# Unread padding in on-chip memory: where the two operands of a split float32 product begin

## What is computed

```python
hx = rmsnorm(x, norm_w[l]) * (1.0 + scale_x[:, None, :]) + shift_x[:, None, :]
(fx, fgx, nqx, nkx, nvx, ngx, gqx, gkx, gvx, ggx, zfx, zbx) = jnp.split(hx @ w_in[l], IN_SPLITS, axis=-1)
...
mix_x = jnp.concatenate([four_x * jax.nn.silu(fgx), na_x * jax.nn.silu(ngx), gla_x * jax.nn.silu(ggx)], axis=-1)
x_new = x + gate_x[:, None, :] * (mix_x @ w_out[l])
```

```python
z = jnp.einsum('bsd,de->bse', a, w_in[i])
...
h = h + jnp.einsum('bse,ed->bsd', mixed, w_out[i])
gate = jax.nn.sigmoid(jnp.einsum('bsd,de->bse', _rmsnorm(h, g_ple[i]), w_ple_gate[i]) + b_ple_gate[i])
h = h + gate * jnp.einsum('bsp,pd->bsd', p[i], w_ple_proj[i])
```

## Time and profile before

| | |
|---|---|
| median of 3 runs | 4333.1 us (4327.89 to 4334.98) |
| span of the profiled execution (first to last instruction) | 4326.4 us |
| TensorE matmuls busy | 3967.8 us, 92% of the span |
| TensorE weight loads busy (beside the matmuls) | 3241.8 us, 75% |
| VectorE, ScalarE, GpSimd busy | 2036.2, 1432.6, 683.4 us (47%, 33%, 16%) |
| DMA moved | 525.90 MB, mean 122 GB/s |

### The profile page before, as it was taken

How to read it: one execution, slowest core, us unless ns; L and a number is a source line. 1 busy time by engine, 2 the same in 40 slices (tenths; PEclk the granted TensorE clock), 3 DMA queues, 4 the chain that set the end, 5 groups by cost and what they waited for, 6 DMA issues and landing times. The chain is left out here.

```text
span 4326.4 us, 66533 instructions
## 1 busy us (share of the span) xinstructions
PE 3967.8 (92%) x25359; PEld 3241.8 (75%) x25359; DVE 2036.2 (47%) x4616; ACT 1432.6 (33%) x3255; POOL 683.4 (16%) x761
## 2 busy tenths in 40 slices
PE   6999999899679799999999869799999989979799
PEld 4777789777568688778977658677777867868687
DVE  5365111167656542111127567632750456657554
ACT  5000444256422310144327523321111467721211
POOL 3021000223120210000032220131430001000100
PEclk8999999999889899999999989899999989989899
DMA  5244221731256422222273345432111143357221
GB/s 195 90 147 143 82 77 61 230 136 59 100 196 220 175 100 73 95 76 77 75 240 106 113 146 198 173 112 90 64 71 66 47 134 102 103 214 255 79 77 64
DMA packets 215264, 525.90 MB, mean 122 GB/s; under 512 B 27478, under 2 KB 88392, under 8 KB 205604
## 3 DMA queue, kind: packets, MB, share of 16 engines
q1 hardware_dynamic: 188740, 438.91, 29.2%
q0 software_dynamic: 26208, 82.74, 5.4%
HBM read 330.43 MB, written 191.13 MB: 121 GB/s over the span
## 5 line engine op out<-in xcount | busy, mean ns | idle before, releaser
L72 PE MATMUL tm_tacc<-tm_tw_hi,hT_hi 128*128 128x384 f32 (+1 forms) x1120 | 414.6, 370 | 17.2 <-DVE tm_tw_lo L906 10.0
L73 PE MATMUL tm_tacc<-tm_tw_lo,hT_hi 128*128 128x384 f32 (+1 forms) x1120 | 410.0, 366 | 0.0
L74 PE MATMUL tm_tacc<-tm_tw_hi,hT_lo 128*128 128x384 f32 (+1 forms) x1120 | 410.0, 366 | 0.0
L72 PE MATMUL tz_tacc<-tz_tw_hi,hT_hi 128*128 128x512 f32 x896 | 359.4, 401 | 6.0 <-POOL tz_tw_lo L935 4.1
L72 PE MATMUL cm_acc<-hT_hi,cm_wb_hi 128*128 128x512 f32 (+1 forms) x912 | 362.2, 397 | 0.0
L73 PE MATMUL tz_tacc<-tz_tw_lo,hT_hi 128*128 128x512 f32 x896 | 355.0, 396 | 0.0
L74 PE MATMUL tz_tacc<-tz_tw_hi,hT_lo 128*128 128x512 f32 x896 | 355.0, 396 | 0.0
L74 PE MATMUL cm_acc<-hT_hi,cm_wb_lo 128*128 128x512 f32 (+1 forms) x912 | 344.3, 378 | 0.0
L73 PE MATMUL cm_acc<-hT_lo,cm_wb_hi 128*128 128x512 f32 (+1 forms) x912 | 343.9, 377 | 0.0
L788 DVE SCALAR_TENSOR_TENSOR tm_ds<-tm_dg,tm_ds 128x512 f32<-128x512 f32 (+1 forms) x40 | 25.6, 639 | 532.1 <-ACT tm_ds L782 532.1
L72 PEld LDWEIGHTS tm_tacc<-tm_tw_hi,hT_hi 128*128 128x128 f32 x1120 | 210.9, 188 | 59.1 <-DVE tm_tw_lo L906 13.6
(11 more groups left out here) (405 smaller groups left out, 8770.1 us busy)
## 6 DMA issues: line engine op xcount, KB each, us to landing
scr_z<-tz_tz SPq DMA_DIRECT2D x112, 256.0 KB
scr_zcm<-cm_zo SPq DMA_DIRECT2D x96, 256.0 KB, 2.0
scr_ztm<-tm_tz SPq DMA_DIRECT2D x68, 256.0 KB, 2.0
scr_xres<-out_x POOLq DMA_DIRECT2D x34, 512.0 KB, 4.1
cm_area<-in_w_ada POOLq DMA_DIRECT2D x64, 256.0 KB, 3.0
scr_z<-out_xn POOLq DMA_DIRECT2D x32, 512.0 KB, 4.8
mo_z<-scr_z SPq DMA_DIRECT2D x16, 1024.0 KB
tz_traw<-in_w_in SPq DMA_DIRECT2D x7, 2048.0 KB, 8.4
```

Of the source, the lines that this page charges most:

```text
L72: nc.tensor.matmul(out, ah, bh, start=start, stop=False)
L73: nc.tensor.matmul(out, ah, bl, start=False, stop=False)
L74: return nc.tensor.matmul(out, al, bh, start=False, stop=stop)
```

## The change

Three kinds of unread buffers are allocated, each a few dozen to 256 bytes per partition, so that later buffers begin elsewhere. `pad_to` pads until the next buffer begins a wanted number of bytes above the other operand, modulo 512: 256 everywhere, but 96 in `tz`. `edge` moves the buffers at the right-hand end down by 96 bytes, which brings `wo_lo` to the residue of `wo_hi`. No instruction is added, removed or moved, on any engine, and no transfer.

```diff
+LINE = 512
+EDGE = 96
+
+
+def residue(nc):
+
+    return (nc.sbuf_base + 31) // 32 * 32 % LINE
+
+
+def pad_to(nc, name, at, apart=256):
+
+    gap = (at + apart - residue(nc)) % LINE
+    if gap:
+        nc.alloc_sbuf_tensor(f"{name}_pad", [128, gap // 4], F32)
+
...
-    def __init__(self, alloc, name, shape):
+    def __init__(self, alloc, name, shape, at=None):
+        self.at = at
...
     raw = [P.sb(f"raw{j}", [128, KC, 128]) for j in range(2)]
+    pad_to(nc, f"{P.name}_wb", hT.at)
     wb = [Split(P.sb, f"wb{j}", [128, KC, 128]) for j in range(2)]
...
     raw, w_in = first.raw, first.w_in
+    pad_to(nc, f"{P.name}_tw", hT.at, 96 if turn else 256)
     wb = Split(P.sb, "tw", [128, KC, width])
...
         right = lambda n, shape: self.nc.alloc_sbuf_tensor(f"{P.name}_{n}", shape, F32, side="right")
+        right("edge", [128, EDGE // 4])
...
+            nc.alloc_sbuf_tensor(f"wl{l}_edge", [128, EDGE // 4], F32, side="right")
             self.lo_rows = [nc.alloc_sbuf_tensor(f"wo{l}_lo{j}", [128, LT], F32R, side="right") for j in range(KC // 2)]
...
+        self.at = residue(nc)
         self.hi = P.sb("hi", [128, KC, D], F32R)
...
+        pad_to(nc, f"{P.name}_mT", wo.at)
         mT = [Split(P.sb, f"mT{j}", [128, KC, 128]) for j in range(2)]
...
+        pad_to(nc, f"{P.name}_hT", fw.wo.at)
         hT = [Split(P.sb, f"hT{j}", [128, KC, 128]) for j in range(2)]
```

More of the change, by code:

```diff
@@ L2430, in __init__ @@
     def __init__(self, P):
-        self.wo = Split(P.sb, "wo", [128, KC, D])
+        self.wo = Split(P.sb, "wo", [128, KC, D], residue(P.nc))
         self.raw_in = [P.sem(f"raw_in{j}") for j in range(2)]
@@ L3146, in second_block @@
     with nc.cleanup_on_exit():
-        hT = Split(nc.alloc_sbuf_tensor, "hT2", [128, KC, LX])
+        hT = Split(nc.alloc_sbuf_tensor, "hT2", [128, KC, LX], residue(nc))
         order = [2, 3, 0, 1, 4, 5, 6]
@@ L3176, in first_layer @@
         with nc.cleanup_on_exit():
-            hT = Split(nc.alloc_sbuf_tensor, f"hT_{l}", [128, KC, LT])
+            hT = Split(nc.alloc_sbuf_tensor, f"hT_{l}", [128, KC, LT], residue(nc))
             with phase(nc, f"cm{l}") as P:
```

## The result

The changed kernel takes 4303.08 us (median of 4 runs, 4300.26 to 4307.91) against 4334.04 for the kernel before (4 runs, 4327.89 to 4336.56). The ratio is 0.9934, 95% interval 0.992 to 0.9948: 31 us or 0.7% faster, within 0.3% of the 4291 us forecast, with 11 us less gain than the 41.9 of the sum. The profiled execution of after is its slowest run (4307.91, span 4306.1), that of before its fastest (4327.89, span 4326.4).

A forecast was written before the change was run, and what follows sets the result against it. The prediction took TensorE's matmul stream as the bound; gains of 7.6 + 10.8 + 7.2 + 5.1 + 2.3 + 8.9 = 41.9 us took 4333.1 to 4291.2 us. The range over the cases was 4218 to 4346.

The forecast's parts named there:

- What bounds: Stages with split products: only TensorE's matmul stream sets the time, so a nanosecond per matmul is one of the kernel.
- That the distance of the starts makes the pace: Split products: the distance between both operands' starts sets the pace, as 6.6 ns between the two layers of `cm`.
- nothing changes: Rival, all stages: starts don't matter, something else such as VectorE's traffic parts the `cm` layers; 4333 us, chance 0.20.
- my form of it: Split products: the next matmul's weight load and the running matmul's stream hinder each other reading on-chip memory; no separate size.
- 226.7 at 256: Split products of 512 columns: distance 256 runs at 226.7 ns, the best level of the trace, chosen between 220.1 and 233.3.
- a level further down: Rival, split products: 256 removes one more step, pace 220.1 ns; 108.5 us gained, 4225 us, chance 0.22.
- Slower: Rival, split products: 256 is like its neighbour 224, all stages at 233.3 ns; 13.5 us lost, 4346.6 us, chance 0.20.
- `tm`, `out`, `mo`: These stages reach 226.7 ns at 512 columns: 10.8, 7.2 and 5.1 us gained; 384 columns in `tm` gain 0.
- `tz`: Stage `tz`, at its new distance: between nothing and a full level of 17.7 us; the middle, 8.9 us, taken.
- `cm` of layer 0: `cm`, layer 0: 1152 matmuls gain 6.6 ns each, 7.6 us.
- `fin`: Stage `fin`: 704 matmuls go from 230.0 to 226.7 ns, 2.3 us; the small `plT` products left out.
- The likeliest case: All stages: best level of the trace, 226.7 ns at 256; 4291 us, own range 4271 to 4300, chance 0.38.

The follow-up runs named there:

- only_tz0: Kernel before with 64 unread bytes ahead of the moving operand in `tz` alone, bringing it to distance 0: 4319.65 us, ratio 0.9974.
- tz0: Changed kernel with distance 0 instead of 96 bytes in `tz`: 4290.42 us, ratio to the kernel before 0.9899.
- both_moved: Kernel before with every left-hand buffer 96 bytes further on, distances kept except for `wo_lo` in `out`: 4339.27 us, ratio 1.0013.
- the two sweeps: Changed kernel with other distances of the operands' starts in each stage, dealt differently in two kernels: 4335.75 and 4338.29 us, one run each.
- low_half: Changed kernel with 320 unread bytes between the halves of `mT` in `out` and `mo`, low half at distance 64: 4312.53 us.
- half_load: Changed kernel with `mo` at distance 224 and 64 of 128 stationary columns loaded for six of eight slices in `out` and `mo`: 4297.31 us.
- fine: Changed kernel with the stationary operand further on by 4 and 8 bytes in `out` (layers 0, 1), 16 in `mo`, 24 in `fin`: 4306.97 us.

## Why the prediction was right, step by step

- **What bounds: right.** TensorE's stream set the end. `only_tz0` turned 17.7 us of pace into 12.4 us of kernel time, `tz0` into 15.5.
- **That the distance of the starts makes the pace: right, and shown** by `both_moved` (addresses change, paces stay), by `only_tz0` (one distance, one stage) and by the two sweeps. VectorE's traffic, which the rows could not exclude, is excluded by them: the stages keep their instructions and change their pace. With this the rival *nothing changes* has fallen. The Trainium skill says in "TensorE: Matmul & The Clock Gate", Step-by-step, that the two operands have independent read ports and that a load takes nothing from the stream. If that were all, there would be no place for 6.6 ns per matmul that hang on the distance of the two starts alone, and the measurement decides. *How* the two accesses meet, in a port or elsewhere, isn't shown: `low_half` refuted my form of it, `half_load` and `fine` fit neither theory.
- **226.7 at 256: right to a tenth of a ns, for half a reason.** I chose it because the distances on both sides of 256, 192 and 0, were good. The sweeps show that the period is 256, so that 256 is the same distance as 0, which rows 6 had already priced. The rival *a level further down* had no room after that: there is no farthest distance at 256. *Slower* compared 256 with its neighbour 224, on a curve where a neighbour says nothing.
- **`tm`, `out`, `mo`: right** in pace, and 1.7, 1.4 and 0.6 us short in time. That 384 columns were already one level lower held in most of the stream, 173.3 at 256 too, but not in all: the earlier trace rows missed the stretches at 176.7. By my estimate from the traces, 267 and 513 such matmuls in the two profiles of before at 3.4 ns each, some 1.3 of the 9.1 us of `tm` come from them and not from 512 columns.
- **`tz`: the step that failed.** I wrote that nothing decides between nothing and a level, and took the middle, 8.9 us. Measured: 0.1. With the period of 256 known, 416 is 160, and rows 5 gave its price, 233.3. The mean of `out` at 231.1 misled me, because it mixes distances of 0 and 416 over three matmuls. As `low_half` showed, one bad operand out of three gives the same mean of 231.1: it costs 4.4 ns on the mean of three, not a third of 6.6.
- **`cm` of layer 0: 7.6 forecast, 2.8 seen.** The pace is there. By the unrounded starts of the first profile of each kernel, intervals up to 260 ns add up to 7.2 us less, and the longer ones to 3.0 more; 8 intervals went over from the first kind to the second. Part of these are the matmuls of the row sums, which wait for VectorE. The groups of before and then of after, 90 to 470 us (in the idle column, DVEq is VectorE's sequencer):

```profile
L328 PE MATMUL cm_msums<-cm_mones,cm_area 128*128 128x1 f32 x64 | 7.7, 250 | 1.4 <-DVEq L353 1.4
L319 PE MATMUL cm_msums<-cm_area,cm_mpick 128*2 128x512 f32 x8 | 4.1, 596 | 2.4 <-DVEq L353 2.4
```

```profile
L345 PE MATMUL cm_msums<-cm_mones,cm_area 128*128 128x1 f32 x64 | 7.7, 250 | 1.8 <-DVEq L370 1.8
L336 PE MATMUL cm_msums<-cm_area,cm_mpick 128*2 128x512 f32 x8 | 4.1, 592 | 3.6 <-DVEq L370 3.6
```

  The two waits go from 3.8 to 5.4 us, and in the second pair of profiles from 3.9 to 5.3: VectorE did not get faster, so a matmul that comes earlier waits longer for it. That is 1.6 of the 3.0 us; the rest has no name.
- **`fin`: 2.3 forecast, 5.1 seen.** With `hT` 24 bytes off, at 230.0, `fine` has 255.3 us in this stage against 251.6, so 3.7 us hang on that distance. From start to start the products of `hT` give 3.3 us (177.3 to 174.0), 1 more than the pace alone. Those of `plT`, which I had left out, changed their distance as well and give 1.1 (41.0 to 39.9), and the wait ahead of the transposes gives the 0.3 to 0.8 that are left.
- **The sum.** The stages give 27.0 us where 41.9 were forecast: 8.8 is `tz`, 4.8 `cm` of layer 0, 0.3 `cm` of layer 1, 3.8 are `tm`, `out` and `mo`, and `fin` returned 2.8. The medians differ by 31 and 26 us in the two comparisons.

The likeliest case held, though its own range (4271 to 4300) missed the time by 3 us. That `tz0` lands at 4290, on the forecast, is chance: it has 17.7 us of pace in `tz` where the forecast had 8.9, and less elsewhere.

## What to carry to other kernels

Where matmuls follow each other without a gap, divide the distance of two starts by the matmuls between them; the mean duration hides a difference of 3%. If two stages with the same shapes have different paces, compare where their two operands begin, modulo 256 here, before looking at anything that moves, and try distance 0, measured at your own number of columns, since at 256 columns another one was better. 32 to 256 unread bytes per stage were worth 1% of this kernel. And when a table of prices over some parameter is rough, look for its period before choosing a value between neighbours.

## What the runs showed of the hardware

- The pace of 128x128 by 128x512 split products depends on the distance of the operands' starts modulo 256 bytes: 226.7 ns at 0; 228.9 to 230.0 at 192; 231.5 to 234.3 at 32, 64, 96, 128, 160 and 224. At 384 columns it is 173.3 at 0, 96 and 192, 175.9 at 128, and at 224 either 173.3 or 176.7, changing along the stream. At 256 columns it is 120.0 at 0 and 160, some 118.5 at 32 and 128, and 113.3 at 64.
- At distance 0 the paces of 512, 384 and 256 columns (226.7, 173.3, 120.0) lie on one line: 53.3 or 53.4 ns for each 128 columns, and some 13.3 ns on top.
- 4 bytes off cost 5.7 ns (232.4), 8 bytes 3.9 (230.6), 16 bytes nothing (226.7), 24 bytes 3.3 (230.0).
- With the stationary operand of the third matmul off (`out` of `low_half`), the intervals are 228.7, 229.3 and 235.0 ns; with the moving operand of the second off (`out` before), 232.6, 231.7 and 229.3. The mean is 231.1 both times.
- A stationary operand of 64 columns instead of 128, at distance 256, made the pace worse: 230.0 instead of 226.7 ns. The weight load lasts 190 ns at 128 columns, 135 at 64 and 85 at 2 (`cm_msums`).
